# Low-weight passes of a unit gathered behind its other passes, with TensorE's wait for the low weights moved there

## The chip, the cores and the metric

One NeuronCore of a Trainium2 chip runs the whole program in one launch. The metric is the time on the device in microseconds, the median of the runs. The engines named in this document are TensorE (PE; its weight loads have rows of their own, PEld), VectorE (DVE), ScalarE (ACT), GpSimd (POOL) and SyncE (SP), which starts the transfers of the weights.

## What is computed

Two transformer blocks in fp32, on 256 tokens of width 1024. The first is a feed-forward block, a mixer (sparse attention and an S5 scan side by side), a second feed-forward block and a gated embedding. The second has two layers, each with a retention, a gated MLP and a differential attention between `w_in` and `w_out`; its first layer also carries 256 context tokens, so that many of its products have 512 columns.

```python
def swiglu(x, w1, w3, w2):
    return (jax.nn.silu(x @ w1) * (x @ w3)) @ w2
...
    # first_block
    h = h + 0.5 * swiglu(rmsnorm(h, norm_ffn1[i]), ffn1_w1[i], ffn1_w3[i], ffn1_w2[i])
    z = rmsnorm(h, norm_mix[i]) @ w_in[i]
    ...
    h = h + jnp.concatenate([o_nsa, o_s5], axis=-1) @ w_out[i]
    h = h + 0.5 * swiglu(rmsnorm(h, norm_ffn2[i]), ffn2_w1[i], ffn2_w3[i], ffn2_w2[i])
    gate = jax.nn.sigmoid(rmsnorm(h, norm_ple[i]) @ w_ple_gate[i])
    h = h + gate * (p[i] @ w_ple[i])
    ...
    # second_block, each layer l
    h = modulate(x, g_pre[l], shift, scale)
    rk_, rv_, dk_, dv_, rq_, rg_, dq_, dg_, mu_, mv_, mg_, mlog_ = split_cols(h @ w_in[l], IN_SIZES)
    ...
    out = merge_branches(o_ret, o_mlp, o_diff, mlog_, w_branch_out[l], w_out[l])
    x = x + gate * rms_norm(out, g_post[l])
```

The feed-forward width is 2816, so each feed-forward block has 22 columns of tiles f.

## The kernel before

**Units.** All weights come as a stream of 359 units of 128 x 1024 fp32 (512 KB); a unit is eight 128 x 128 tiles, and `stream_plan` gives their order. In a feed-forward block that is w1 and w3 of column f = 0, then for each f the w1 and w3 of f + 1 and the w2 of f. SP loads unit u into slot u % 4 of `ring` (four slots) and waits for that until PE has multiplied unit u - 4 (`units_multiplied`, raised by the last matmul of a unit).

**Three passes.** For 347 of the units, the split ones, an fp32 product is made of three passes with fp32r operands. ACT copies the unit into its high part `w_hi` (`high_part`, L1290; three slots; it waits for the load and for the multiplying of the split unit three before). DVE then subtracts, `w_lo` = `ring` - `w_hi` (`low_part`, L451; it waits for the high part and raises `lo_ready`). The input is likewise kept as a high and a low part: `hn` (high part on ACT at L1365 or L1575, low part on DVE at L1897 or L2309) and `hid` in the feed-forward (`hid_hi` on ACT, `hid_lo` at L2015 on DVE). `exact` (L518 to L525) gives the three passes of a tile one after the other: `w_hi` x high input, `w_hi` x low input, `w_lo` x high input. A unit is thus 24 passes, of 256 or 512 columns.

**PE's waits.** Before a unit PE waits for its low part (`split_unit`, L512 to L516), and so implicitly for its high part:

```python
def split_unit(name, body=0):
    who, count = LOW[name]
    pe.wait_ge(lo_ready[who], count + body)
    return w_parts(name)
```

**Order of work.** PE's order is that of the stream. ACT's order of high parts (`part`, `prepare`) and DVE's of low parts are written out by hand between their other steps: on DVE in a feed-forward block as `part(3 * f + 2)`, `gated`, `part(3 * f + 3)`, `gated_low`, with steps of the S5 tables (L1937 to L1975) and of the modulation (`mod_junk`, L1919) between them, and elsewhere as `low_until(name)`, which makes all low parts up to the named unit. `modulated` (L2300) is the loop over the eight tiles of a normalised input: L2306 scales a tile, ACT makes its high part (`hn_hi`), L2309 its low part (`hn_lo`); its argument `lows` names a tile behind which a low part of weights is made. It is called with `{7: ("dk", l, 2)}` for layer 0 and with `{5: ("dq", l, 2)}` for layer 1. `head_sum` puts a small product between two tiles of `project2`.

**Where the three passes are used.** `up` and `down` in the feed-forward blocks (and `first_up` for their first two units), `project` for the projections of block 1, the units `wout`, `context_half`, `residual_halves`, `project2` for the projections of block 2 (`ctx_by_tile` for one unit that waits for its input tile by tile), and the units `wbo` and `wo` at the end of each layer.

## Time and profile before

| | |
|---|---|
| median of 3 runs | 1518.09 us (1516.82 to 1519.3) |
| profiled execution | 1522.82 us, span 1521.1 us |
| mean granted TensorE clock in it | 0.996 |
| PE busy | 1465.7 us (96%), 10,040 matmuls |
| DVE busy | 959.2 us (63%) |
| ACT busy | 721.5 us (47%) |
| transfers | 223.25 MB, mean 147 GB/s |
| chain that ended last | PE 80%, DVE 8%, DMA 6%, ACT 4% |

A row of the timeline gives the start, the duration, engine, line and operation, then what is written and what is read, and in brackets the idle time of the engine before it with what ended it. The ends of matmuls are modelled: the distance between two starts says more than a duration. The execution goes through feed-forward 1 (to 212 us), the projections and the mixer (to 364), feed-forward 2 (to 554), the gated embedding and the change to block 2 (to 620), and the two layers of block 2, of which the second begins at about 1150.

### The profile page before, as it was taken

How to read it: one execution, taken by the hardware profiler on the slowest of the kernel's cores; microseconds unless marked ns; L12 is line 12 of the kernel's file. 1: busy time of each engine (PE TensorE's matmuls, PEld its weight loads, DVE VectorE, ACT ScalarE, POOL GpSimd, SP SyncE). 2: the span in 40 equal slices, each digit the busy share in tenths (PEclk: the TensorE clock that was granted, in tenths of full speed). 3: DMA queues.
4: the chain of work that ended last, by engine and by line, in shares of the span. 5: the costliest groups of instructions: out<-in, count | busy, mean ns of one | idle time of the engine just before them, and what ended most of it. 6: DMA issues, size and time to landing. Idle time of an engine off the chain costs nothing.

```text
span 1521.1 us, 25975 instructions
## 1 busy us (share of the span) xinstructions
PE 1465.7 (96%) x10040; PEld 1304.4 (86%) x10040; DVE 959.2 (63%) x1522; ACT 721.5 (47%) x1252; POOL 80.6 (5%) x129
## 2 busy tenths in 40 slices
PE   6999999989999999999999999999999999999997
PEld 6999999769999988787778788888888887889997
DVE  5778788767666678865654447664246635557665
ACT  5444466366444457327545353222245435556444
POOL 4600000000000000001001000000000002010000
PEclk9999999999999999999999999999999999999999
DMA  7766645516666644442222123543332332225663
GB/s 277 236 197 194 211 134 199 176 49 228 223 211 207 217 159 147 159 159 77 70 70 70 56 83 133 177 134 111 101 108 97 99 124 77 83 94 180 210 206 130
DMA packets 71033, 223.25 MB, mean 147 GB/s; under 512 B 6688, under 2 KB 21024, under 8 KB 70432
## 3 DMA queue, kind: packets, MB, share of 16 engines
q1 hardware_dynamic: 54528, 194.67, 38.7%
q10 hardware_dynamic: 16416, 27.34, 5.4%
q8 instruction: 62, 1.02, 0.3%
q14 instruction: 27, 0.22, 0.0%
HBM read 220.94 MB, written 1.05 MB: 146 GB/s over the span
## 4 chain that ended last, share of the span: by engine, by line
PE 80%; DVE 8%; DMA 6%; ACT 4%; issue 2%; SPq 0%; DVEq 0%; ACTq 0%
PE ps L524 67%; DMA ring<-stream 5%; DVE w_lo L451 3%; ACT w_hi L1290 2%; PE ps L539 1%; PE ps L1029 1%; PE ps L1045 1%; PE ps L1037 1%; DVE mod_junk L1919 1%; PE ps L1113 1%; PE ps L1102 1%; PE ps L1002 1%; PE ps L1082 0%; DMA pk<-pack 0%; PE ps L1062 0%
## 5 line engine op out<-in xcount | busy, mean ns | idle before, releaser
L524 PE MATMUL ps<-hn_hi,w_hi 128*128 128x256 f32 (+1 forms) x1895 | 603.3, 318 | 17.2 <-DVE w_lo L451 9.8
L451 DVE TENSOR_TENSOR w_lo<-ring,w_hi 128x1024 fp32r<-128x1024 f32 (+1 forms) x347 | 415.1, 1202 | 283.2 <-ACT w_hi L1290 279.5
L524 PE MATMUL ps<-hn_hi,w_lo 128*128 128x256 f32 (+1 forms) x1895 | 589.5, 311 | 0.0
L524 PE MATMUL ps<-hn_lo,w_hi 128*128 128x256 f32 (+1 forms) x1895 | 589.1, 311 | 0.0
L1290 ACT ACTIVATE w_hi<-ring 128x1024 fp32r<-128x1024 f32 (+1 forms) x347 | 360.2, 1039 | 339.5 <-DMA ring<-stream 263.6
L524 PEld LDWEIGHTS ps<-hn_hi,w_hi 128*128 128x128 f32 x1895 | 359.1, 189 | 47.1 <-DVE w_lo L451 15.5
L524 PEld LDWEIGHTS ps<-hn_lo,w_hi 128*128 128x128 f32 x1895 | 360.1, 190 | 20.7 <-issue 0.5
L524 PEld LDWEIGHTS ps<-hn_hi,w_lo 128*128 128x128 f32 x1895 | 358.3, 189 | 21.3
L1359 ACT ACTIVATE area<-ps 128x512 f32<-128x512 f32 (+1 forms) x136 | 67.1, 508 | 209.3 <-PE ps L524 209.0
L524 PE MATMUL ps<-area_r,w_hi 128*128 128x256 f32 (+1 forms) x578 | 132.1, 323 | 0.9 <-ACT area L1359 0.6
L524 PE MATMUL ps<-hid_hi,w_hi 128*128 128x256 f32 x352 | 99.3, 282 | 6.5 <-DVE w_lo L451 5.2
L524 PEld LDWEIGHTS ps<-area_r,w_hi 128*128 128x128 f32 x578 | 95.9, 188 | 11.1 <-DVE w_lo L451 1.1
L524 PE MATMUL ps<-hid_lo,w_hi 128*128 128x256 f32 x352 | 97.7, 278 | 0.0
L524 PE MATMUL ps<-hid_hi,w_lo 128*128 128x256 f32 x352 | 97.7, 277 | 0.0
L524 PE MATMUL ps<-area_r,w_lo 128*128 128x256 f32 (+1 forms) x289 | 92.7, 321 | 0.0
L524 PE MATMUL ps<-w_hi,hn_hi 128*128 128x512 f32 (+1 forms) x192 | 77.3, 402 | 0.0
L524 PEld LDWEIGHTS ps<-hid_hi,w_hi 128*128 128x128 f32 x352 | 66.2, 188 | 8.8 <-issue 6.0
L524 PE MATMUL ps<-w_lo,hn_hi 128*128 128x512 f32 (+1 forms) x192 | 73.4, 382 | 0.0
L524 PE MATMUL ps<-w_hi,hn_lo 128*128 128x512 f32 (+1 forms) x192 | 73.3, 382 | 0.0
L524 PEld LDWEIGHTS ps<-hid_hi,w_lo 128*128 128x128 f32 x352 | 66.2, 188 | 0.0
L524 PEld LDWEIGHTS ps<-hid_lo,w_hi 128*128 128x128 f32 x352 | 66.2, 188 | 0.0
L524 PEld LDWEIGHTS ps<-area_r,w_lo 128*128 128x128 f32 x289 | 54.3, 188 | 4.5
(328 smaller groups left out, 1568.1 us busy)
## 6 DMA issues: line engine op xcount, KB each, us to landing
ring<-stream SPq DMA_DIRECT2D x359, 512.0 KB, 3.8
mod_at<-mod_stream ACTq DMA_DIRECT2D x24, 512.0 KB, 5.4
area<-mod_stream ACTq DMA_DIRECT2D x22, 512.0 KB, 4.9
pk<-pack ACTq DMA_DIRECT2D x1, 1610.0 KB, 7.2
pk<-pack SPq DMA_DIRECT2D x1, 1549.0 KB, 12.2
h<-x_in SPq DMA_DIRECT2D x1, 1024.0 KB, 4.8
cond_at<-cond SPq DMA_DIRECT2D x2, 512.0 KB, 14.2
mod_at<-mod_stream SPq DMA_DIRECT2D x2, 512.0 KB, 12.5
```

What stands on the lines that cost most here:

```text
L451: eng.tensor_tensor(lo[:, 0:w], raw, hi[:, 0:w].bitcast(F32), ALU.subtract).then_inc(lo_ready[who], 1)
L524: m = pe.matmul(dst, w_, x_, start=(start and n == 0), stop=(stop and n == 2), skip_group_check=True)
L539: m = pe.matmul(bank(b, 0, tokens), c("ones"), src, start=(k == first), stop=(k == KT - 1), skip_group_check=True)
L1002: m = pe.matmul(ps[:, 4 * 512 + T * j:4 * 512 + T * j + T], c("rot64" if part[0] == "d" else "rot128"), z[:, a0 + j, 0:T], start=(j % 2 == ...
L1029: pe.matmul(bank(4 + m_, T * st, 2 * T - T * st), diffz[rows, 4 + hh, q0:q0 + P], diffz[rows, hh, keys], start=True, stop=True).then_inc(s ...
L1037: m = pe.transpose(bank(6, P * kt, P), aux[:, 4 + n % 2, P * kt:P * kt + P], c("ident"))
L1045: m = pe.matmul(bank(7, P * qt, P), diffv[:, kt, P * hh:P * hh + P], aux[:, 6 + n % 2, P * kt:P * kt + P], start=(kt == 2 * st), stop=(kt ...
L1102: m = pe.matmul(bank(4 + n % 2, T * kt, T), retz[:, hh, T * st + P * kt:T * st + P * kt + P], retz[:, 4 + hh, T * st:T * st + T], start=(k ...
L1113: m = pe.matmul(bank(6 + n % 2, 0, T), retv[:, 2 * st + kt, P * hh:P * hh + P], aux[:, n % 2, T * kt:T * kt + T], start=(kt == 0), stop=(s ...
L1290: act.activation(w_parts(name)[0][:, 0:w], ring[:, u % RING, PLACE:PLACE + w], ACT.Copy).then_inc(hi_ready, 1)
L1359: act.activation(dst, bank(BANK[name][0], 0, tokens), func, **kw).then_inc(act_evac, 1)
L1919: stt(quarter(mod_junk[:, :].bitcast(BF16)), w, 1.0, silu(0), ALU.mult, ALU.mult, accum_out=out_at(0)).then_inc(s("mod_half"), 1)
```

## The change

For 259 of the 347 split units PE no longer waits for the low part at the head. It waits for the high part (`high_unit`), gives the two passes with `w_hi` for all eight tiles (`high_passes`), then waits for the low part (`low_unit`) and gives the eight passes with `w_lo` (`low_pass`). These are the units of `up` and `down` (128), those of `project`, `wout` from 2 on and `pleg`, `context_half`, and those of `project2` but for the one with `ctx_by_tile`. `first_up`, `residual_halves`, `wbo`, `wo` and the units in which the input is the stationary operand stay as they are. On DVE the low part of ("dk", 0, 2) and that of ("dq", 1, 2) are moved from inside the two `modulated` loops to behind them. `head_sum` stands behind as many passes as before. The hunks for `wout` and `context_half` are like that of `project` and left out here.

```diff
@@ -515,6 +515,26 @@
                 pe.wait_ge(lo_ready[who], count + body)
                 return w_parts(name)
 
+            def high_unit(name, body=0):
+
+                pe.wait_ge(hi_ready, SPLIT[name] + 1 + body)
+                return w_parts(name)
+
+            def low_unit(name, body=0):
+
+                who, count = LOW[name]
+                pe.wait_ge(lo_ready[who], count + body)
+
+            def high_passes(dst, weights, wcols, x, xcols, start):
+
+                for n in range(2):
+                    m = pe.matmul(dst, weights[0][wcols], x[n][xcols], start=(start and n == 0), stop=False, skip_group_check=True)
+                return m
+
+            def low_pass(dst, weights, wcols, x, xcols, stop):
+
+                return pe.matmul(dst, weights[1][wcols], x[0][xcols], start=False, stop=stop, skip_group_check=True)
+
             def exact(dst, weights, wcols, x, xcols, start, stop, x_stationary=False):
...
@@ -560,18 +580,26 @@
 
                 def up(f, body=0):
                     for half, w in enumerate(("w1", "w3")):
-                        wt = split_unit((tag, w, f), body)
+                        wt = high_unit((tag, w, f), body)
                         for k in range(KT):
-                            m = exact(bank(4 + f % 4, T * half, T), wt, (all_p, slice(P * k, P * k + P)),
-                                      hn, (all_p, k, slice(0, T)), k == 0 and half == 0, k == KT - 1)
+                            high_passes(bank(4 + f % 4, T * half, T), wt, (all_p, slice(P * k, P * k + P)),
+                                        hn, (all_p, k, slice(0, T)), k == 0 and half == 0)
+                        low_unit((tag, w, f), body)
+                        for k in range(KT):
+                            m = low_pass(bank(4 + f % 4, T * half, T), wt, (all_p, slice(P * k, P * k + P)),
+                                         hn, (all_p, k, slice(0, T)), k == KT - 1)
                         m.then_inc(units_multiplied, 1)
 
                 def down(f, body=0, hidden=0):
-                    wt = split_unit((tag, "w2", f), body)
+                    wt = high_unit((tag, "w2", f), body)
                     pe.wait_ge(hidden_ready, FT * n_ffn + f + 1 + hidden)
                     for j in range(KT):
-                        m = exact(bank(j // 2, T * (j % 2), T), wt, (all_p, slice(P * j, P * j + P)),
-                                  hid, (all_p, f % 4, all_t), f == 0 and j % 2 == 0, f == FT - 1)
+                        high_passes(bank(j // 2, T * (j % 2), T), wt, (all_p, slice(P * j, P * j + P)),
+                                    hid, (all_p, f % 4, all_t), f == 0 and j % 2 == 0)
+                    low_unit((tag, "w2", f), body)
+                    for j in range(KT):
+                        m = low_pass(bank(j // 2, T * (j % 2), T), wt, (all_p, slice(P * j, P * j + P)),
+                                     hid, (all_p, f % 4, all_t), f == FT - 1)
                     m.then_inc(units_multiplied, 1)
...
@@ -603,16 +631,18 @@
             def project(name, tokens=T, cols=None, kt=KT, src=None):
 
                 split = name in SPLIT
-                wt = split_unit(name) if split else unit(name)
+                wt = high_unit(name) if split else unit(name)
                 bank_free(pe, name)
-                b = BANK[name][0]
-                for k in range(kt):
-                    if split:
-                        m = exact(bank(b, 0, tokens), wt, (all_p, slice(P * k, P * k + P)), hn, (all_p, k, slice(0, tokens)),
-                                  k == 0, k == kt - 1)
-                    else:
-                        m = pe.matmul(bank(b, 0, tokens), wt[:, P * k:P * k + P], src[:, k, 0:tokens],
-                                      start=(k == 0), stop=(k == kt - 1))
+                o = bank(BANK[name][0], 0, tokens)
+                if split:
+                    for k in range(kt):
+                        high_passes(o, wt, (all_p, slice(P * k, P * k + P)), hn, (all_p, k, slice(0, tokens)), k == 0)
+                    low_unit(name)
+                    for k in range(kt):
+                        m = low_pass(o, wt, (all_p, slice(P * k, P * k + P)), hn, (all_p, k, slice(0, tokens)), k == kt - 1)
+                else:
+                    for k in range(kt):
+                        m = pe.matmul(o, wt[:, P * k:P * k + P], src[:, k, 0:tokens], start=(k == 0), stop=(k == kt - 1))
                 m.then_inc(units_multiplied, 1)
...
@@ -963,15 +999,26 @@
 
 
             def project2(name, l, tokens, ctx_by_tile=False):
-                wt = split_unit(name)
+                wt = high_unit(name)
                 bank_free(pe, name)
                 o = bank(BANK[name][0], 0, tokens)
-                for k in range(KT):
-                    if ctx_by_tile:
+                if ctx_by_tile:
+                    low_unit(name)
+                    for k in range(KT):
                         pe.wait_ge(s("ctx_modulated"), KT * l + k + 1)
-                    m = exact(o, wt, (all_p, slice(P * k, P * k + P)), hn, (all_p, k, slice(0, tokens)), k == 0, k == KT - 1)
-                    if k == (3 if tokens > T else 5):
-                        head_sum()
+                        m = exact(o, wt, (all_p, slice(P * k, P * k + P)), hn, (all_p, k, slice(0, tokens)), k == 0, k == KT - 1)
+                        if k == 3:
+                            head_sum()
+                else:
+                    for k in range(KT):
+                        high_passes(o, wt, (all_p, slice(P * k, P * k + P)), hn, (all_p, k, slice(0, tokens)), k == 0)
+                        if tokens > T and k == 5:
+                            head_sum()
+                    low_unit(name)
+                    for k in range(KT):
+                        m = low_pass(o, wt, (all_p, slice(P * k, P * k + P)), hn, (all_p, k, slice(0, tokens)), k == KT - 1)
+                        if tokens <= T and k == 1:
+                            head_sum()
                 m.then_inc(units_multiplied, 1)
...
@@ -2463,12 +2510,13 @@
                 tok = 2 * T if l == 0 else T
                 dve.wait_ge(mods_ready, 4 + 3 * l)
                 if l == 0:
-                    modulated(0, 0, h, lambda k: gamp[:, k:k + 1], aux[:, 9, T:2 * T], {7: ("dk", l, 2)})
+                    modulated(0, 0, h, lambda k: gamp[:, k:k + 1], aux[:, 9, T:2 * T])
+                    low_until(("dk", l, 2))
                     final_norm()
                 else:
                     low_until(("dq", l, 1))
                     dve.wait_ge(s("x_rstd"), 2)
-                    modulated(1, 0, h, lambda k: amp[:, 1, k, 0:1], rstd[:, 0:T], {5: ("dq", l, 2)})
+                    modulated(1, 0, h, lambda k: amp[:, 1, k, 0:1], rstd[:, 0:T])
                     low_until(("dq", l, 3))
```

## Rows read from the trace of the kernel before

**Rows 1.** Busy time by engine, share of the span, instructions: the page.

```profile
PE 1465.7 (96%) x10040; PEld 1304.4 (86%) x10040; DVE 959.2 (63%) x1522; ACT 721.5 (47%) x1252; POOL 80.6 (5%) x129
```

**Rows 2.** PE's waits (us, times, longest): 0:212, 212:364, 364:554, 554:620, 1150:1521.

```profile
PE ps L524 <- DVE w_lo L451: 5.3, 8, 1.7
PE ps L524 <- DVE hid_lo L2015: 1.1, 1, 1.1
...
PE ps L524 <- DVE w_lo L451: 1.4, 2, 1.0
...
PE ps L524 <- DVE w_lo L451: 3.6, 7, 0.8
...
PE ps L524 <- DVE w_lo L451: 2.8, 4, 1.0
PE ps L524 <- DVE hn_lo L2309: 1.8, 1, 1.8
...
PE ps L524 <- DVE w_lo L451: 2.0, 4, 0.8
PE ps L524 <- DVE hn_lo L2309: 1.4, 1, 1.4
```

**Rows 3.** Groups by shape: busy, mean ns, idle time before and its releasers.

```profile
L451 DVE TENSOR_TENSOR w_lo<-ring,w_hi 128x1024 fp32r<-128x1024 f32 x331 | 404.4, 1227 | 261.7 <-ACT w_hi L1290 258.0
...
L1290 ACT ACTIVATE w_hi<-ring 128x1024 fp32r<-128x1024 f32 x331 | 350.1, 1059 | 325.7 <-DMA ring<-stream 254.2 <-PE ps L524 61.7 <-issue 9.1
```

**Rows 4.** Timeline of PE, 67 to 76 us (start, duration, work, idle before).

```profile
67.23 0.28 PE L524 MATMUL ps<-hid_hi,w_lo 128*128 128x256 f32 x1
...
67.84 0.38 PE L524 MATMUL ps<-hn_hi,w_hi 128*128 128x256 f32 x1 [0.33 <-DVE w_lo L451]
68.06 0.29 PE L524 MATMUL ps<-hn_lo,w_hi 128*128 128x256 f32 x1
...
70.57 0.28 PE L524 MATMUL ps<-hn_hi,w_lo 128*128 128x256 f32 x1
70.68 0.28 PE L524 MATMUL ps<-hn_hi,w_hi 128*128 128x256 f32 x1
...
75.30 0.38 PE L524 MATMUL ps<-hid_hi,w_hi 128*128 128x256 f32 x1 [1.74 <-DVE w_lo L451]
```

**Rows 5.** Chain of waits, 60 to 130 us (start, duration, what).

```profile
81.39 4.44 DMA ring<-stream
85.86 1.07 ACT w_hi L1290
```

**Rows 6.** Timeline of DVE, 66 to 77 us.

```profile
66.56 1.23 DVE L451 TENSOR_TENSOR w_lo<-ring,w_hi 128x1024 fp32r<-128x1024 f32 x1 [2.18 <-ACT w_hi L1290]
...
73.21 0.69 DVE L1975 TENSOR_SCALAR area<-area 128x1024 f32<-128x1024 f32 x1
```

**Rows 7.** Timeline of PE, 50 to 51.2 us.

```profile
50.80 0.28 PE L524 MATMUL ps<-hn_hi,w_lo 128*128 128x256 f32 x1
50.92 0.28 PE L524 MATMUL ps<-hn_hi,w_hi 128*128 128x256 f32 x1
```

**Rows 8.** Timeline of PE, 208 to 209 us.

```profile
208.62 0.39 PE L524 MATMUL ps<-hid_hi,w_hi 128*128 128x256 f32 x1 [0.85 <-DVE w_lo L451]
```

**Rows 9.** Timeline of ACT, 205 to 232 us.

```profile
212.43 2.54 ACT L1272 ACTIVATE area<-h 128x256 f32<-128x256 f32 x8
```

**Rows 10.** Busy times in one stretch, then granted clock, DMA share, GB/s.

```profile
601.20:604.60 3.40, 3.40 (x18) 3.40 (x17) 3.06 (x9) 2.77 (x5) 0.00 (x0) 0.50 0.79 317
```

**Rows 11.** Timeline of DVE, 1160 to 1166 us.

```profile
1163.26 1.22 DVE L451 TENSOR_TENSOR w_lo<-ring,w_hi 128x1024 fp32r<-128x1024 f32 x1 [0.34 <-ACT w_hi L1290]
```

**Rows 12.** Timeline of DVE, 603 to 608 us.

```profile
605.93 1.22 DVE L451 TENSOR_TENSOR w_lo<-ring,w_hi 128x1024 fp32r<-128x1024 f32 x1
```

**Rows 13.** Timeline of ACT, 611 to 614 us.

```profile
612.68 1.05 ACT L1290 ACTIVATE w_hi<-ring 128x1024 fp32r<-128x1024 f32 x1
```

**Rows 14.** Weight loads of PE, 70.3 to 70.9 us.

```profile
70.57 0.19 PEld L524 LDWEIGHTS ps<-hn_hi,w_hi 128*128 128x128 f32 x1
```

More of the change, by code:

```diff
@@ L906, in _ @@
             for j in range(2, KT):
-                wt = split_unit(("wout", j))
+                wt = high_unit(("wout", j))
                 bank_free(pe, ("wout", j))
                 for k in range(KT):
-                    m = exact(bank(BANK["wout", j][0], 0, T), wt, (all_p, slice(P * k, P * k + P)),
-                              hn, (all_p, k, slice(0, T)), k == 0, k == KT - 1)
+                    high_passes(bank(BANK["wout", j][0], 0, T), wt, (all_p, slice(P * k, P * k + P)), hn, (all_p, k, slice(0, T)), k == 0)
+                low_unit(("wout", j))
+                for k in range(KT):
+                    m = low_pass(bank(BANK["wout", j][0], 0, T), wt, (all_p, slice(P * k, P * k + P)),
+                                 hn, (all_p, k, slice(0, T)), k == KT - 1)
                 m.then_inc(units_multiplied, 1)
@@ L944, in context_half @@
                 for k in range(KT):
-                    exact(bank(BANK[name][0], T, T), wt, (all_p, slice(P * k, P * k + P)),
-                          hn, (all_p, k, slice(T, 2 * T)), k == 0, k == KT - 1)
+                    high_passes(bank(BANK[name][0], T, T), wt, (all_p, slice(P * k, P * k + P)), hn, (all_p, k, slice(T, 2 * T)), k == 0)
+                low_unit(name)
+                for k in range(KT):
+                    low_pass(bank(BANK[name][0], T, T), wt, (all_p, slice(P * k, P * k + P)),
+                             hn, (all_p, k, slice(T, 2 * T)), k == KT - 1)
             def residual_halves(names):
@@ L965, in project2 @@
             def project2(name, l, tokens, ctx_by_tile=False):
-                wt = split_unit(name)
+                wt = high_unit(name)
                 bank_free(pe, name)
                 o = bank(BANK[name][0], 0, tokens)
-                for k in range(KT):
-                    if ctx_by_tile:
+                if ctx_by_tile:
+                    low_unit(name)
+                    for k in range(KT):
                         pe.wait_ge(s("ctx_modulated"), KT * l + k + 1)
-                    m = exact(o, wt, (all_p, slice(P * k, P * k + P)), hn, (all_p, k, slice(0, tokens)), k == 0, k == KT - 1)
-                    if k == (3 if tokens > T else 5):
-                        head_sum()
+                        m = exact(o, wt, (all_p, slice(P * k, P * k + P)), hn, (all_p, k, slice(0, tokens)), k == 0, k == KT - 1)
+                        if k == 3:
+                            head_sum()
+                else:
+                    for k in range(KT):
+                        high_passes(o, wt, (all_p, slice(P * k, P * k + P)), hn, (all_p, k, slice(0, tokens)), k == 0)
+                        if tokens > T and k == 5:
+                            head_sum()
+                    low_unit(name)
+                    for k in range(KT):
+                        m = low_pass(o, wt, (all_p, slice(P * k, P * k + P)), hn, (all_p, k, slice(0, tokens)), k == KT - 1)
+                        if tokens <= T and k == 1:
+                            head_sum()
                 m.then_inc(units_multiplied, 1)
```

## The prediction

> **What bounds the kernel now.** I read the page's busy times first [rows 1]. TensorE (PE) is busy for 1465.7 of 1521.1 us, so whatever the change can win lies in the 55 us in which PE is idle, or in the pace of its passes. Next come the waits of PE, one answer for each stage [rows 2]. Every row "w_lo L451" is PE standing at the head of a weight unit for its low part: 5.3 + 1.4 + 3.6 + 2.8 + 2.0 = 15.1 us in 8 + 2 + 7 + 4 + 4 = 25 waits; between 620 and 1150 us there is none. The other rows are two waits for the low part of the input (hn_lo L2309) and one for hid_lo. The third view is the groups by shape [rows 3]: making a high part takes ACT 1.06 us, and the low part takes VectorE (DVE) another 1.23 us after it, since the subtraction reads the high part.
>
> What a wait costs is more than its idle figure, because the ends of matmuls are modelled. At 67.23 the last pass of a unit starts, and at 67.84 the next [rows 4]: 0.61 us where two passes are 0.11 us apart, so 0.50 is lost though the row says 0.33. The following start is at 68.06, 0.22 later and not 0.11: the restart takes another 0.11. So a wait costs its idle time plus 0.17 plus 0.11, about 0.27 us more than listed. All 25 together: 15.1 + 25 x 0.27 = 21.9 us. That is the pot.
>
> The chain of waits shows where such a wait comes from [rows 5]: once a unit has left the ring, the load of the next takes 4.44 us, and its high part follows at 85.86 for 1.07 us; the low part comes behind that. DVE has two sorts of delay [rows 6]: it is in other work when the high part is ready (73.21 is a table step, and only behind it comes the low part for which PE waits until 75.30), or the high part itself is just done (66.56, idle before, released by w_hi). In the second sort PE loses at most the 1.23 us of the low part.
>
> **The change part by part.** *Low part asked for 16 passes later.* A unit has 24 passes. In 259 of the 347 split units (128 of the two feed-forward blocks, 24 of the other projections before block 2, 107 of block 2) the first 16 now need only the high part. At 0.113 to 0.118 us a pass for 256 columns [rows 4, 7] the low part may now be 1.8 to 1.9 us later than before, at 512 columns 3.6 us later. The largest listed wait is 1.7 idle [rows 2], so 2.0 in all: nearly all waits fit under the new allowance. The number of passes, their columns, the weight loads, the order of units and the moment at which a unit is released are unchanged; a unit is released by its last pass as before, and the DMA queue of SP, which waits for that, sees the same order. Where PE now waits in the middle of a unit, what stands behind it are 8 passes and, at the end, the release that frees a ring slot, so a late low part delays the load four units on as it does today.
>
> *High part asked for at the head.* It is ready 1.2 us or more ahead of the low part. I take each stage by itself (idle + 0.27 a wait):
> - Feed-forward 1, to 212 us: 5.3 + 8 x 0.27 = 7.5. The last of its waits (208.62, idle 0.85, so 1.1 in all [rows 8]) brings nothing: ACT begins the squares at 212.43 with no idle before them [rows 9], so ACT is the bound there, and PE needs the squares. Around 75.30 DVE is held by its table steps, so I leave 0.5 there. 5.9 remain. The hid_lo wait (1.1) stays, since hid_lo stands behind the same low part on DVE.
> - 212 to 364: 1.4 + 2 x 0.27 = 1.9, of which I take 1.7 (0.3 of it stands ahead of ACT and DVE chains of the attention, which keep their length).
> - Feed-forward 2, 364 to 554: 3.6 + 7 x 0.27 = 5.5, all of it; the units before and behind are on time.
> - 554 to 620: 2.8 + 4 x 0.27 = 3.9. Here DVE is the rival bound: PE already waits 1.8 us for hn_lo [rows 2], at 600.89, so arriving earlier there mostly makes this wait longer. Behind it lies a stretch in which the granted clock is 0.50 [rows 10], the lower of the two levels (1.2 GHz), in which 18 passes take 3.40 us; it came after that idle time and would stay, since the idle time does.
> - From 1150: 2.0 + 4 x 0.27 = 3.1; the last of the four (0.2 idle, so 0.5) stands before a unit whose order isn't changed, and I leave another 0.3. I take 2.3.
>
> *Low parts taken out of the two normalisation loops.* At 1163.26 DVE makes the low part of a later unit between two tiles of hn_lo [rows 11], and PE waits 1.4 us for the next tile [rows 2]. The step takes 1.22 us; ACT has its own high part in between, so 1.2 comes back, with the low part then made behind the loop and needed 16 passes later. At 605.93 it is the same for the last tile of the other loop [rows 12], but PE is then still at the tiles before it, so I take 0.3, a quarter of the step. Behind it the unit at 615.04 needs its high part, which ACT makes from 612.68 to 613.73 [rows 13] behind DVE steps that keep their length: with the low part waiting in the middle, PE could start there at most 1.3 earlier, and this takes the place of the 0.3. With an estimated 0.8 where PE sums squares earlier, the stage brings 2.1 of its 3.9. Cover of this edit: DVE does the same steps in all; without the 16 passes of cover each low part would cost its 1.23 us again.
>
> *The extra wait itself.* 259 units get one wait more. Lower end: zero, and not below, since a met wait removes nothing: as between two units of one kind when the semaphore is already there: starts at 70.57 and 70.68, 0.11 apart, across a unit's end [rows 4]. Upper end: a full restart, 0.107 us, 259 times = 27.7 us. I take zero: it is the same situation, one wait on one semaphore in front of a weight load. The Trainium skill's page "TensorE: Matmul & The Clock Gate" (Part 2, step by step) says that weight loads are pulled ahead of the matmuls in flight. A wait in front of a load could stop that, and the sum by that reading would be 18.7 - 27.7 = -9.0. By this trace the load for the pass at 70.68 starts at 70.57 [rows 14], together with the pass before it, so there loads go on being pulled ahead past a met wait.
>
> *Pace.* Passes of 256 columns run at two paces: 0.113 (70.57 to 70.68 [rows 4]) and 0.118 (50.80 to 50.92 [rows 7]), and stay in one until a unit's end. Of the intervals between starts on L524 (the rows of its timeline from 15.28 on), 2,194 are at most 0.115 us and 3,139 are 0.116 to 0.119, with means of 0.1134 and 0.1178. All three kinds of pass keep whichever pace the unit has, so I see no reason for a shift by their order. Bounds: all at the fast one -3,139 x 0.0044 = -13.8 us; all at the slow one +2,194 x 0.0044 = +9.7. I take zero and keep a part of both ends.
>
> **Sum.** 5.9 + 1.7 + 5.5 + 2.1 + 2.3 + 1.2 = 18.7 us. The profiled execution took 1522.8 us (span 1521.1), so 1504.1 there; the median of the runs shown is 1518.1, 4.7 lower, and the same subtraction gives **1499.4 us**.
>
> **Rivals.**
> - *The next thing is late.* Where PE comes sooner, ACT or the DMA is what it meets. A load takes 4.44 us and the high part 1.07 [rows 5]; a slot is refilled three units ahead of its use, 3 x 24 x 0.113 = 8.1 us, so 2.6 us are spare. For it: a fifth of ACT's idle time ahead of high parts is no wait for a load (325.7 in all, 254.2 for loads) [rows 3], and several stages hang on ACT. If half of the pot comes back, 21.9 / 2 = 11, the time is 1507.
> - *Pace moves in our favour.* Mid-unit there is no switch between w_hi and w_lo any more, and half of the slow passes could turn fast: 7 us more, 1492. Against it: nothing in the rows ties pace to the kind of pass.
> - *Each mid-unit wait is a restart.* Mechanism: the wait drains the queue of loads even when it is met; place: between pass 16 and 17 of each of the 259 units. 27.7 - 18.7 = +9.0, so 1527. It decides from 0.072 us per unit (18.7 / 259). For it: the restart of 0.107 is real after a wait that was not met. Against it: 70.57 to 70.68 [rows 4, 14].
> - *It doesn't do what it says*: the waits move to the middle of the unit instead of vanishing, because DVE falls behind by what PE gains. Then 1515 to 1520. Against it: DVE stands idle for 258.0 us waiting for high parts [rows 3].
>
> **How the numbers follow.** Forecast (13 to 22 us won) 0.55; next thing late (4 to 13) 0.20; pace in favour (over 22) 0.12; restarts or a slower pace, above 1521 0.07; no effect 0.06. About 0.2%, 3.0 us, is what a measurement here can tell from no change. Faster by more than that: 0.55 + 0.20 + 0.12 = 0.87; within 0.06; slower 0.07. Range: forecast, the better part of "late" and most of the pace case, 1490 to 1512, leaves about 2 in 10 outside.
>
> **What would show it.** In the changed profile: PE's waits for w_lo fall from 25 to a handful, all in front of a pass hn_hi,w_lo; the wait at 600.89 grows to 3 us or more; the hn_lo wait of the 1150 stage all but goes; in a unit whose low part is ready, passes 16 and 17 start 0.11 to 0.12 apart (0.22 would be the restart rival); the counts of the two paces stay. Wrong it would be if new waits for w_hi L1290 of several us appear, or if the mean of the low passes rises by itself.

## The result, and the profile after

| | before | changed |
|---|---|---|
| median | 1518.07 us (1516.82 to 1519.3, 4 runs) | 1503.04 us (1502.62 to 1503.81, 4 runs) |
| profiled execution | 1522.82 us, span 1521.1 | 1502.62 us, span 1500.8 |

The ratio is 0.9902, with a 95% interval of 0.9885 to 0.9919: the change takes 15.0 us off the median. Between the two profiled executions the difference is 20.3 us of span: the profiled run of before lay 4.7 us above its median, that of the changed kernel 0.4 below its own.

In the changed kernel the two passes with `w_hi` have line L531, the low passes L536, the units left in the old order L544, the sums of squares L559; the low parts of the weights are still made at L451, the high parts now at L1337, `hid_lo` at L2062, `hn_lo` at L1944 and L2356. From the page of the changed kernel: its span, the busy times, the chain by engine, and the low passes as a group.

```profile
span 1500.8 us, 25976 instructions
PE 1456.7 (97%) x10040; PEld 1300.7 (87%) x10040; DVE 957.8 (64%) x1522; ACT 720.6 (48%) x1252; POOL 85.3 (6%) x129
PE 88%; DVE 5%; ACT 3%; DMA 2%; issue 1%; DVEq 0%; SPq 0%; ACTq 0%
...
L536 PE MATMUL ps<-hn_hi,w_lo 128*128 128x256 f32 (+1 forms) x1720 | 291.7, 312 | 0.5 <-DVE w_lo L451 0.5
```

PE is busy 97% of the time instead of 96 [rows 1]; the chain goes through PE for 88% of the span instead of 80, and through DVE for 5% instead of 8. Behind the low passes, 1,720 of them in this group, PE idled for 0.5 us.

PE's waits over the whole span (us in total, times, longest), those that answer to [rows 2]:

```profile
PE ps L559 <- ACT area L1319: 4.0, 2, 2.4
PE ps L544 <- DVE hn_lo L2356: 2.3, 3, 1.8
PE ps L531 <- ACT w_hi L1337: 1.6, 2, 0.8
PE ps L531 <- DVE hid_lo L2062: 1.5, 2, 0.8
PE ps L536 <- DVE w_lo L451: 0.5, 1, 0.5
PE ps L544 <- DVE w_lo L451: 0.2, 1, 0.2
```

The 25 waits for w_lo, 15.1 us, have become one of 0.5 us in the middle of a unit and one of 0.2 in a unit of the old order. The waits for hn_lo in the two loops, 3.2 us together before, are 2.3 us. New are two waits for a high part, 1.6 us. The waits for squares on ACT, 4.0 us here, were 2.5 in the same two places in the trace of before, and those for hid_lo, 1.5 us in two places, were 1.1 in one.

Rows of PE's timeline of the changed kernel (start, duration, work, idle before):

```profile
69.96 0.28 PE L531 MATMUL ps<-hn_lo,w_hi 128*128 128x256 f32 x1
70.08 1.11 PE L536 MATMUL ps<-hn_hi,w_lo 128*128 128x256 f32 x8
71.02 0.29 PE L531 MATMUL ps<-hid_hi,w_hi 128*128 128x256 f32 x1
...
204.93 1.35 PE L559 MATMUL ps<-area,pk 128*128 128x256 f32 x5 [2.39 <-ACT area L1319]
...
572.11 1.12 PE L559 MATMUL ps<-area,pk 128*128 128x512 f32 x2 [1.07 <-DVE area L1933]
...
585.89 0.39 PE L544 MATMUL ps<-hn_hi,w_hi 128*128 128x256 f32 x1 [1.83 <-DVE hn_lo L2356]
...
599.05 0.50 PE L531 MATMUL ps<-hn_hi,w_hi 128*128 128x512 f32 x1 [0.83 <-ACT w_hi L1337]
...
1148.21 0.39 PE L544 MATMUL ps<-hn_hi,w_hi 128*128 128x256 f32 x1 [0.25 <-DVE hn_lo L2356]
...
1162.57 0.97 PE L536 MATMUL ps<-hn_hi,w_lo 128*128 128x256 f32 x6 [0.53 <-DVE w_lo L451]
```

At 69.96 the sixteenth pass of a unit starts, and at 70.08 the first low one: 0.12 us across the added wait. The other rows are where PE now waits, in the order of time.

**Where the time went.** Each last matmul of a unit raises a semaphore, so the ends of all units can be set beside each other in two traces; they stand in no row of the page and were taken from the traces' semaphore records. The lead of the changed kernel over the profiled run of before is 1.15 us at the first unit (the start, before any changed unit), 9.09 at the end of feed-forward 1, 7.95 at the first unit of the mixer (1.15 lost again in front of the squares), 9.65 at `wout` 4, 14.93 at the end of feed-forward 2, 16.01 at the first units of block 2, 16.01 still at 1150 us, 18.99 at about 1180 and 20.3 at the end. The 1.15 us of the start is not the change's: the first unit ends at 22.15 us in this profile of the changed kernel and at 23.48 in its second one, at 23.30 and at 22.36, 23.41 and 22.18 in the four of before.

### The profile page after: what moved, and what is told of

It is laid out like the page before. It is cut to its first block, busy times and chain, and to the rows that moved or that the text cites. A ratio compares the mean times of both kernels' runs of the same rounds, so it can differ in the third digit from the quotient of the medians.

```text
span 1500.8 us, 25976 instructions
## 1 busy us (share of the span) xinstructions
PE 1456.7 (97%) x10040; PEld 1300.7 (87%) x10040; DVE 957.8 (64%) x1522; ACT 720.6 (48%) x1252; POOL 85.3 (6%) x129
## 4 chain that ended last, share of the span: by engine, by line
PE 88%; DVE 5%; ACT 3%; DMA 2%; issue 1%; DVEq 0%; SPq 0%; ACTq 0%
PE ps L531 37%; PE ps L544 21%; PE ps L536 18%; DMA ring<-stream 1%; PE ps L1076 1%; PE ps L559 1%; PE ps L1092 1%; ACT w_hi L1337 1%; DVE w_lo L451 1%; PE ps L1084 1%; PE ps L1160 1%; PE ps L1149 1%; PE ps L1049 1%; PE ps L1129 0%; DMA pk<-pack 0%
## 5 line engine op out<-in xcount | busy, mean ns | idle before, releaser
L451 DVE TENSOR_TENSOR w_lo<-ring,w_hi 128x1024 fp32r<-128x1024 f32 (+1 forms) x347 | 415.1, 1202 | 268.1 <-ACT w_hi L1337 263.8
L1337 ACT ACTIVATE w_hi<-ring 128x1024 fp32r<-128x1024 f32 (+1 forms) x347 | 360.1, 1039 | 330.0 <-DMA ring<-stream 243.7
L531 PE MATMUL ps<-hn_hi,w_hi 128*128 128x256 f32 (+1 forms) x1720 | 495.5, 317 | 2.7 <-ACT w_hi L1337 1.6
L531 PE MATMUL ps<-hn_lo,w_hi 128*128 128x256 f32 (+1 forms) x1720 | 486.0, 311 | 0.0
L531 PEld LDWEIGHTS ps<-hn_hi,w_hi 128*128 128x128 f32 x1720 | 324.2, 188 | 25.7 <-issue 4.3
L531 PEld LDWEIGHTS ps<-hn_lo,w_hi 128*128 128x128 f32 x1720 | 324.4, 189 | 19.4 <-issue 0.7
L536 PE MATMUL ps<-hn_hi,w_lo 128*128 128x256 f32 (+1 forms) x1720 | 291.7, 312 | 0.5 <-DVE w_lo L451 0.5
L536 PEld LDWEIGHTS ps<-hn_hi,w_lo 128*128 128x128 f32 x1720 | 247.4, 189 | 20.5 <-DVE w_lo L451 0.7
L544 PE MATMUL ps<-area_r,w_hi 128*128 128x256 f32 (+1 forms) x578 | 132.0, 323 | 0.7 <-ACT area L1406 0.4
L544 PEld LDWEIGHTS ps<-area_r,w_hi 128*128 128x128 f32 x578 | 95.9, 188 | 10.6 <-DVE w_lo L451 0.8
L544 PE MATMUL ps<-area_r,w_lo 128*128 128x256 f32 (+1 forms) x289 | 92.7, 321 | 0.0
L531 PE MATMUL ps<-hid_hi,w_hi 128*128 128x256 f32 x352 | 83.0, 278 | 1.5 <-DVE hid_lo L2062 1.5
L531 PE MATMUL ps<-hid_lo,w_hi 128*128 128x256 f32 x352 | 82.5, 277 | 0.0
L544 PE MATMUL ps<-w_hi,hn_hi 128*128 128x512 f32 (+1 forms) x192 | 77.3, 402 | 0.0
L544 PE MATMUL ps<-w_lo,hn_hi 128*128 128x512 f32 (+1 forms) x192 | 73.4, 382 | 0.0
L544 PE MATMUL ps<-w_hi,hn_lo 128*128 128x512 f32 (+1 forms) x192 | 73.3, 382 | 0.0
L531 PEld LDWEIGHTS ps<-hid_hi,w_hi 128*128 128x128 f32 x352 | 66.1, 188 | 1.9 <-issue 0.9
L531 PEld LDWEIGHTS ps<-hid_lo,w_hi 128*128 128x128 f32 x352 | 66.3, 188 | 0.0
L544 PE MATMUL ps<-hn_hi,w_hi 128*128 128x256 f32 (+1 forms) x175 | 55.1, 315 | 5.3 <-DVE hn_lo L1944 2.9
L544 PEld LDWEIGHTS ps<-area_r,w_lo 128*128 128x128 f32 x289 | 54.3, 188 | 4.4
L1325 ACT ACTIVATE lnr<-ps,eps 128x256 f32<-128x256 f32 x34 | 16.1, 473 | 79.4 <-PE ps L1109 48.1
```

Of the source, the lines that this page charges most:

```text
L451: eng.tensor_tensor(lo[:, 0:w], raw, hi[:, 0:w].bitcast(F32), ALU.subtract).then_inc(lo_ready[who], 1)
L531: m = pe.matmul(dst, weights[0][wcols], x[n][xcols], start=(start and n == 0), stop=False, skip_group_check=True)
L536: return pe.matmul(dst, weights[1][wcols], x[0][xcols], start=False, stop=stop, skip_group_check=True)
L544: m = pe.matmul(dst, w_, x_, start=(start and n == 0), stop=(stop and n == 2), skip_group_check=True)
L1325: link(act.activation(lnr[:, col:col + tokens], src, ACT.Ln, bias=eps[:, 0:1], scale=1.0 / width))
L1337: act.activation(w_parts(name)[0][:, 0:w], ring[:, u % RING, PLACE:PLACE + w], ACT.Copy).then_inc(hi_ready, 1)
```

## Experiments

Each kernel stands beside runs of the kernel before from its own chip and its own comparison. The ratio is not always the quotient of the two medians: for the kernels below the two can be 1 us apart, so a gain is given by both where it matters.

**Order or wait.** The first three kernels have the same order of passes and differ only in where PE asks for the low part: ahead of pass 1, of pass 9 or of pass 17 (the changed kernel itself).

```diff
             def high_unit(name, body=0):
 
-                pe.wait_ge(hi_ready, SPLIT[name] + 1 + body)
+                who, count = LOW[name]
+                pe.wait_ge(lo_ready[who], count + body)
                 return w_parts(name)
 
             def low_unit(name, body=0):
 
-                who, count = LOW[name]
-                pe.wait_ge(lo_ready[who], count + body)
+                pass
```

> The changed kernel with its order of passes and its two moved low parts, but PE waits for the low part at the head of each unit, as before. Theory (the gain is the cover of 16 passes in front of the wait): 1516.5 to 1518.5, at most 1.5 us below before, and the waits for w_lo are back at 20 to 27. Rival (the order of passes itself brings the gain, by pace or by loads of the same tile following one another): 1503 to 1506.

Measured: 1517.96 us beside 1519.92 of before, ratio 0.9994 (0.9979 to 1.0008), with a highest run of 1522.43. The order of the passes alone, with the two moved low parts, can't be told from no change, and is far from the rival's 1503 to 1506. Its waits for w_lo:

```profile
PE ps L531 <- DVE w_lo L451: 11.7, 19, 1.7
PE ps L544 <- DVE w_lo L451: 0.2, 1, 0.2
```

They are back, 20 of them. The two kernels differ in nothing but the place of the wait, so the gain is the wait's, not the order's.

```diff
                         for k in range(KT):
+                            if k == 4:
+                                low_unit((tag, w, f), body)
                             high_passes(bank(4 + f % 4, T * half, T), wt, (all_p, slice(P * k, P * k + P)),
                                         hn, (all_p, k, slice(0, T)), k == 0 and half == 0)
-                        low_unit((tag, w, f), body)
```

(and so in `down`, `project`, `wout`, `context_half` and `project2`)

> The changed kernel with the wait for the low part in front of the ninth pass of a unit (behind tile 3's high passes) and not in front of the seventeenth; the order of the passes is that of the changed kernel. Theory: a cover of 8 passes, 0.91 us at 256 columns. Of the losses in the profile of before only four were longer than that where the low part was what PE needed: 1.90, 1.19, 1.10 and 0.99 us, of which 0.98, 0.27, 0.18 and 0.07 would be left, each with a restart of 0.11: 1.9 us. So 1504 to 1505.5. Rival (each unit loses in proportion to how early it waits): half of the 15 us, 1510 to 1511.

Measured: 1506.25 us beside 1519.92, ratio 0.9917 (0.9896 to 0.9937): with half of the cover 13.7 us of gain by the medians and 12.6 by the ratio, and no run above 1508.25, so the rival's 1510 to 1511 is out. What is left of the waits, and the largest of them:

```profile
PE ps L531 <- DVE w_lo L451: 2.2, 4, 0.6
...
72.72 0.38 PE L531 MATMUL ps<-hid_hi,w_hi 128*128 128x256 f32 x1 [0.63 <-DVE w_lo L451]
```

Four waits, 2.2 us listed and 3.3 with 0.27 each, where 1.9 were expected. The ends of the units show them: they fall behind those of the changed kernel by 0.9 us at 75, 0.4 at 225 and 0.8 at 570, three of the four losses named, and by 0.8 at 1160 in place of the one of 0.99; another 1.4 lies at 215, behind a half-clock stretch at 205.8. The time is 0.8 above the range; before is 1.9 above its first median in this comparison. Cover is worth what it spans of each wait, and with 0.9 us most of the waits are already gone: a wait of 0.6 us and one of 1.9 are both "a wait for the low part", but only the second needs the other eight passes.

**The added waits.**

```diff
                         low_unit((tag, w, f), body)
                         for k in range(KT):
+                            low_unit((tag, w, f), body)
                             m = low_pass(bank(4 + f % 4, T * half, T), wt, (all_p, slice(P * k, P * k + P)),
```

> The changed kernel with its wait for the low part repeated in front of each of the eight low passes, 259 x 8 = 2,072 more waits, all of them met when they are reached. Theory (a met wait costs nothing): within 2 us of the changed kernel, and starts of low passes stay 0.11 to 0.12 us apart. Rival (a met wait drains the loads, the price at which the prediction's restart case would have decided is 0.072 us): 2,072 x 0.072 = 149 us more, at a full restart of 0.107 us 222 us more.

Measured: 1503.56 us beside 1518.69, ratio 0.9897 (0.9882 to 0.9911): the gain of the changed kernel, 15.1 us, is all there. From its page and its waits:

```profile
span 1502.3 us, 26242 instructions
...
PE ps L536 <- DVE w_lo L451: 0.3, 1, 0.3
```

The span is 1.5 us above that of the changed kernel, against the 149 or 222 us of the restart case; by the ends of the units 1.7 us are lost at 217, behind a half-clock stretch at 206.1. In the trace, starts of low passes of 256 columns are 116.4 ns apart on the mean, in the changed kernel 116.3 (the few above 130 ns left out), and a weight load starts 3 ns behind the start of the pass before it in both, with a wait on it or without. So a met wait in front of a weight load costs under a nanosecond, even if the whole 1.5 us is put down to the 2,072 of them.

The page has 26,242 instructions where that of the changed kernel has 25,976, 266 more and not 2,072. In the trace all 2,072 low loads carry a wait of their own, and 259 instructions are new at the line of `low_unit`, one for each unit: a single wait rides on the weight load, and only in front of the first low pass, where two now stand, is there an instruction of its own. The other 7 belong to the unit with `ctx_by_tile`, where the edit put 8 more waits beside those for the input tiles. The Trainium skill says that of waits on several engines (Perfetto Trace Analysis, Identifying Dependency Chains: such instructions may have an EventSemaphore instruction put ahead of them); here the 259 came with two waits on one semaphore. The changed kernel against the kernel before, with one wait more per unit, has one instruction more. That settles the restart rival, and with it what I had weighed against the Trainium skill's rule on loads pulled ahead (TensorE: Matmul & The Clock Gate, Part 2, Step-by-step): in this trace met waits don't hold the pull-ahead back.

**The two moved low parts.** Once put back in the changed kernel, once moved alone.

```diff
-                    modulated(0, 0, h, lambda k: gamp[:, k:k + 1], aux[:, 9, T:2 * T])
-                    low_until(("dk", l, 2))
+                    modulated(0, 0, h, lambda k: gamp[:, k:k + 1], aux[:, 9, T:2 * T], {7: ("dk", l, 2)})
...
-                    modulated(1, 0, h, lambda k: amp[:, 1, k, 0:1], rstd[:, 0:T])
+                    modulated(1, 0, h, lambda k: amp[:, 1, k, 0:1], rstd[:, 0:T], {5: ("dq", l, 2)})
```

> The changed kernel with the low parts of (dk,0,2) and (dq,1,2) back inside the two loops. Theory: the loop of layer 1 delays hn_lo by 1.2 us, PE waits 1.4 us there again; the loop of layer 0 costs 0.3: 1.2 to 1.5 us above the changed kernel on the same chip. Rival (with the wait behind 16 passes the place of a low part no longer matters): within 0.4 us of it.

Measured: 1503.9 us beside 1502.67 of the changed kernel on the same chip, with overlapping runs (1502.97 to 1504.76 and 1502.32 to 1506.7) and profiled spans of 1501.2 and 1500.9: the times alone don't decide between the theory and the rival. The trace tells more than the medians. PE's timeline with the low parts in the loops:

```profile
1147.68 0.39 PE L544 MATMUL ps<-hn_hi,w_hi 128*128 128x256 f32 x1 [1.39 <-DVE hn_lo L2356]
```

The wait of 1.4 us for hn_lo is back; in the changed kernel it was 0.25 at 1148.21. By the ends of the units, against the second profile of the changed kernel, this is worth 1.17 us. In layer 0 there is nothing to gain: there the changed kernel gains 0.83 us at ("dk", 0, 0) and has lost 1.07 again at ("dk", 0, 3), whose high part comes late (the wait at 599.05).

The move alone, on the kernel before, is the same diff the other way round:

> The kernel before with nothing but the two low parts moved behind the loops; PE waits at the head and takes the passes tile by tile as before. Theory: hn_lo of the layer 1 loop is 1.2 us earlier, and the low part of (dq,1,2) is made behind the loop and still in time, so 0.5 to 1.5 us below before, which these medians can hardly tell from nothing; in the trace PE's wait for hn_lo L2309 at some 1165 falls from 1.4 to under 0.4. Rival (the move pays only with the cover of 16 passes): the waits for w_lo behind the two loops grow by as much.

Measured: 1517.89 us beside 1518.69, ratio 0.9994 (0.9981 to 1.0006), no difference by the medians, as expected. PE's timeline behind the loop of layer 1, the kernel before first:

```profile
1165.33 0.39 PE L524 MATMUL ps<-hn_hi,w_hi 128*128 128x256 f32 x1 [1.40 <-DVE hn_lo L2309]
1172.58 0.38 PE L524 MATMUL ps<-hn_hi,w_hi 128*128 128x256 f32 x1 [0.76 <-DVE w_lo L451]
1176.13 0.38 PE L524 MATMUL ps<-hn_hi,w_hi 128*128 128x256 f32 x1 [0.56 <-DVE w_lo L451]
1179.67 0.38 PE L524 MATMUL ps<-hn_hi,w_hi 128*128 128x256 f32 x1 [0.54 <-DVE w_lo L451]
...
1160.59 0.39 PE L524 MATMUL ps<-hn_hi,w_hi 128*128 128x256 f32 x1 [0.25 <-DVE hn_lo L2309]
1167.84 0.39 PE L524 MATMUL ps<-hn_hi,w_hi 128*128 128x256 f32 x1 [0.75 <-DVE w_lo L451]
1171.38 0.38 PE L524 MATMUL ps<-hn_hi,w_hi 128*128 128x256 f32 x1 [0.54 <-DVE w_lo L451]
1174.92 0.39 PE L524 MATMUL ps<-hn_hi,w_hi 128*128 128x256 f32 x1 [0.55 <-DVE w_lo L451]
```

The wait for hn_lo fell from 1.4 to 0.25, and the three waits for w_lo behind it kept their size. The move doesn't need the cover of 16 passes.

**The feed-forward alone.** `up` and `down` as in the changed kernel, all else as before.

> Only the 128 units of the two feed-forward blocks are gathered; all else is as before, the two low parts inside the loops included. Theory: by the marks of the unit ends in the two profiles, feed-forward 1 gave 6.8 us (without the start) and feed-forward 2 4.9, so 11.7 of 20.3; the median moved by 15.0, so by the same share 8.6 to 11.7 us, 1506.5 to 1509.5. Rival (the feed-forward's gain depends on what follows): under 5 us, above 1513.

Measured: 1510.55 us beside 1519.92, ratio 0.9946 (0.9926 to 0.9966): 9.4 us by the medians, 8.2 by the ratio. The first is in the range expected (8.6 to 11.7), the second just below it; the time is above its range, since before took 1.9 us more in this comparison. It is 55 to 62% of the whole. The rest was not split by runs; its parts are read from the ends of the units.

**How much there is to lose in a run of before.** The changed kernel and the kernel before, again:

> The changed kernel, unchanged, on the chip of the following runs. Theory: 1502.5 to 1505, 15 us below before, whose runs spread over 8 us, and itself spread over less than 3, because a run can no longer lose the w_lo waits. Rival: as wide a spread as that of before (8 us), if the spread has nothing to do with these waits.

Measured: 1502.67 us beside 1516.96, ratio 0.991 (0.9893 to 0.9927). Four of its five runs lie between 1502.3 and 1502.8, one at 1506.7; the nine of before between 1514.9 and 1520.3. That one run, which has no profile, makes the spread 4.4 us, above the 3 expected, beside 5.4 of before. The other kernels with the late wait spread over 1.8 (e3), 4.7 (e7) and 5.2 us (e9), so it is not shown that the change makes the times steadier.

> The kernel before, unchanged, for a second profile. The changed kernel's span is 20.3 us shorter than that of the first profile of before, but its median is only 15.0 us below the median. Theory: the first profile of before lost some 4.7 us in the pot itself (low parts later than usual), so a second one shows fewer or shorter waits of PE for w_lo, some 11 us listed in place of 15.1. Rival: the 4.7 us lie outside these waits (the start, the pace of the passes, the waits for the statistics), and the w_lo waits come out at 14 to 16 us again.

Measured: 1524.28 us, span 1522.5.

```profile
PE ps L524 <- DVE w_lo L451: 15.9, 26, 1.8
```

The theory failed on this run, and the rival's 14 to 16 us came out: it is slower still than the first profile, and the waits are longer too. So two more followed.

> The kernel before, unchanged, one more profile with its own time. Theory: what a run of before loses in the waits for w_lo differs from run to run, and its time with it: a run below 1518 has under 14 us listed in these waits or one half-clock stretch less (1.7 us each) than the first profile, one above 1521 has 15 or more. Rival: the listed waits are 15 to 16 us whatever the time of the run.

Measured: 1519.27 us, span 1517.5.

```profile
PE ps L524 <- DVE w_lo L451: 14.2, 27, 1.1
```

> The same as the run before it, once more: listed waits for w_lo and half-clock stretches against its own time.

Measured: 1518.38 us, span 1516.7, the run nearest to the median. Neither run lies below 1518 or above 1521, where the theory had put its numbers; the rival's 15 to 16 us whatever the time is out.

```profile
PE ps L524 <- DVE w_lo L451: 12.7, 25, 1.1
```

| run of before | time | waits for w_lo, listed | times | half-clock stretches ahead of the end |
|---|---|---|---|---|
| second | 1524.28 | 15.9 | 26 | 3 |
| first (the prediction's) | 1522.82 | 15.1 | 25 | 2 |
| third | 1519.27 | 14.2 | 27 | 0 |
| fourth | 1518.38 | 12.7 | 25 | 2 |

The four stand in the same order by time and by listed waits. That is weak evidence: the profile of the kernel with only the moved low parts took 1517.8 us with 14.7 us in 24 waits. From the first to the fourth the span falls by 4.4 us, of which 2.4 are the listed waits for w_lo and 1.1 lie ahead of the end of the first unit (23.30 and 22.18 us); the rest was not traced. What there is to win differs from run to run: the wait at 75.30, 1.74 us in the first, is not among those of the fourth, whose longest is 1.1. The half-clock stretches (the granted clock at its lower level) don't follow the time; the kernels with the late wait have none, one or two as well (two in the profile of the changed kernel, none in its second one, with spans of 1500.8 and 1500.9).

**Further along the same road.** What the rows after pointed to was tried on top of the change.

```diff
-                    pe.wait_ge(hidden_ready, FT * n_ffn + f + 1 + hidden)
-                    for j in range(KT):
-                        high_passes(bank(j // 2, T * (j % 2), T), wt, (all_p, slice(P * j, P * j + P)),
-                                    hid, (all_p, f % 4, all_t), f == 0 and j % 2 == 0)
+                    for n, ready in enumerate((s("hid_high"), hidden_ready)):
+                        pe.wait_ge(ready, FT * n_ffn + f + 1 + hidden)
+                        for j in range(KT):
+                            pe.matmul(bank(j // 2, T * (j % 2), T), wt[0][all_p, slice(P * j, P * j + P)],
+                                      hid[n][all_p, f % 4, all_t], start=(f == 0 and j % 2 == 0 and n == 0), stop=False,
+                                      skip_group_check=True)
```

> The changed kernel with the 8 hid_hi passes of a w2 unit first, then the 8 hid_lo passes behind a wait of their own, then the 8 low ones. Theory: the same rule as for the weights (ask for the late operand last): two waits for hid_lo, 1.5 us listed, 1.5 + 2 x 0.27 = 2.0 us with what a wait costs, so 1.5 to 2.0 below the changed kernel on the same chip. Rival: what waits for hid_lo now waits for hid_hi or for the low part, no gain.

Measured: 1500.54 us beside 1502.67 of the changed kernel and 1516.96 of before, ratio to before 0.9893 (0.9876 to 0.9911). No wait for hid_lo is left in its trace. Against the second profile of the changed kernel the ends of the units gain 1.03 us at the first w2 unit and 0.91 at the first of feed-forward 2, which are the two places. The spans of these two profiles differ by 2.1 us, but 1.34 of that is the start, and 0.8 of the gain is lost again behind 1450 us, so their sum fits the medians partly by luck. The runs (1498.93 to 1503.66) overlap with those of the changed kernel: the 2.1 us of the medians are likely and not shown, the 1.9 us in the two places are shown by the traces. Its median is the lowest of the study.

```diff
-            high_parts(2)
             squares(1, h, resid_ready, [k // 2 + 1 for k in range(KT)])
+            high_parts(2)
```

> The kernel e7 with the two high parts that ACT makes ahead of the squares at the end of feed-forward 1 put behind the squares. In the profile of the changed kernel PE waits 2.4 us there for the squares, which begin at 204.48 behind those two high parts (2.00 us), while h is ready from 203.2 on. Theory: the squares start 1.3 to 1.9 us earlier, the root follows 0.3 later than it could: 1.0 to 1.6 us below e7. Rival: the low parts of the units of u then come late by as much, 0.

Measured: 1503.19 us, 2.6 above e7, with runs from 1499.61 to 1504.82, which overlap with those of e7: the expected gain isn't there, and a loss is not shown either. The two profiles (e9's run took 1504.6 us, e7's 1500.54) tell where they part. PE's timeline:

```profile
203.40 0.91 PE L559 MATMUL ps<-area,pk 128*128 128x256 f32 x3 [1.23 <-ACT area L1321]
...
243.64 0.36 PE L531 MATMUL ps<-hn_hi,w_hi 128*128 128x256 f32 x1 [2.23 <-DVE area L2142]
```

The wait for the squares fell from 2.4 to 1.2 us, as expected, and 0.7 of that was left at the first unit of the mixer. Then PE stood 2.2 us at 243.64 for a DVE step (L2142, the rope), a wait that e7 doesn't have. On DVE in between:

```profile
230.52 1.23 DVE L1968 SCALAR_TENSOR_TENSOR mod_junk<-mod_at,cond_at 128x1024 bf16<-128x1024 f32 x1 [0.77 <-DMA mod_at<-mod_stream]
235.09 1.23 DVE L1968 SCALAR_TENSOR_TENSOR mod_junk<-mod_at,cond_at 128x1024 bf16<-128x1024 f32 x1 [0.93 <-DMA mod_at<-mod_stream]
```

DVE waits 0.8 and 0.9 us for weights of the modulation, whose loads ACT starts between its other steps. The e7 trace has neither of these waits, and the rope step L2142 starts there at 240.08 where here it starts at 243.07. So in this run the gain was given back some 40 us later, through work that ACT starts and DVE makes. Another 1.5 us of the difference between the two profiles lies at `wout` 0, behind a half-clock stretch at 307. The rival expected PE to wait for the low parts of u; no such wait is there. Which of ACT's steps came too late was not tried, so this cause is read from the rows and not shown by a run.

## Why the prediction held, and what was off

- **What bounds the kernel.** Right: the gain comes from asking for the low part later, and the order of the passes gave nothing that could be measured (e1). Not all of what the waits cost came back: in the fourth run of before they cost 12.7 + 25 x 0.27 = 19.4 us, and the spans differ by 15.8 with the moved low part in it, because in places another bound stands behind them, as the prediction said.
- **Idle plus 0.27 for a wait.** It held in e7: two waits, 1.6 us listed in the second profile of the changed kernel, make 2.1, and 1.9 came back by the ends of the units. At 75.30, 1.74 + 0.27 = 2.0 was predicted and 2.09 came back.
- **Terms by stage,** against the same profile of before: feed-forward 1 5.9, measured 6.8 (7.95 less the 1.15 of the start); 212 to 364 1.7, measured 1.7; feed-forward 2 5.5, measured 5.3; 554 to 620 2.1, measured 1.1; behind 1150 2.3 + 1.2 = 3.5, measured 3.0 to 1180 and 1.3 behind. In all 19.1 us without the start, for 18.7: nearer than its parts deserve, since 0.9 too little in feed-forward 1 and 1.3 behind 1180, for which there was no term, largely cancel 1.0 and 0.5 too much in the two stages of the loops. The 0.5 that I left at 75.30 was not needed: 16 passes covered all of it. What the last wait of feed-forward 1 was to bring and the squares to take back is in the trace as +1.15 and -1.15, with the wait for the squares grown to 2.39.
- **554 to 620.** I put the loss into the wait for hn_lo at 600.89, which was to grow to 3 us. It stayed at 1.83 (585.89); in its place PE waits 1.07 us at an earlier point, 572.11, for a fold on DVE (L1933) that the squares need, and 0.83 at 599.05 for the high part of ("dk", 0, 3). The bound was DVE as said, the row was another. The 0.3 for the moved low part of layer 0, which did not enter the sum, was wrong (e3: nothing). The half-clock stretch behind this wait, which "would stay", is in neither profile of the changed kernel, and it cost nothing: the first profile of before has it and the third has not, and from 580 to 620 us their unit ends stay 2.7 to 2.8 us apart.
- **The median.** This is the step that was mis-sized, 18.7 for 15.0 us. I took the pot from a profiled run that lay 4.7 us above the median, and subtracted it whole from the median. The pot was itself larger in that run: 15.1 us listed, 12.7 in the run near the median. By the profile of that fourth run and the second one of the changed kernel (from another chip) the spans differ by 1516.7 - 1500.9 = 15.8 us. The row to doubt was in hand: the profiled time stood 4.7 above the median in the same sentence.
- **The extra wait.** Right at zero (e5); the rival needed 0.072 us a unit.
- **Pace.** Of the intervals of 256 columns at most 0.115 us there are 2,037 in place of 2,194, and of 0.116 to 0.119 us 3,366 in place of 3,139: 0.7 to 1.0 us slower. In the second profile of the changed kernel they are 2,129 and 3,267, in the fourth of before 2,115 and 3,241, so most of that shift is the run's and not the change's.
- **The next thing late.** It was there, small: w_hi 1.6 us in two waits, not the half of the pot.

## What to carry to other kernels

Where one operand comes late and the product is a sum of passes, give all passes without it first and wait in the middle: it costs nothing when the operand is there. How much cover is needed is read from the longest waits, not from their sum; here 8 of 16 passes gave 12.6 to 13.7 of 15 us. The waits read from one profiled run belong to that run: where its time lies above the median, don't subtract them whole from the median.

## What the runs showed of the hardware

A wait that is met costs under 1 ns where it rides on a weight load (2,072 of them 1.5 us at most, e5); a second wait on the same load makes an instruction more. Behind a wait that was not met the second pass starts 0.22 us after the first (67.84 and 68.06), where 0.113 is usual [rows 4].

The granted clock fell to half for stretches of 3.41 us with PE at work in them (busy for 3.10 to 3.40 of 3.40 us, in the 18 of them that the 14 profiles have ahead of the end of the program). Here is one behind the longest wait for w_lo in the second run of before, and one behind PE's first wait for hn_lo in the changed kernel; last, a wait of e4 without one. The rows of stretches give busy times, granted clock, DMA share and GB/s:

```profile
73.54 0.38 PE L524 MATMUL ps<-hid_hi,w_hi 128*128 128x256 f32 x1 [1.79 <-DVE w_lo L451]
...
74.20:77.60 3.40, 3.40 (x18) 3.40 (x17) 3.37 (x6) 0.76 (x2) 0.00 (x0) 0.51 0.49 155
...
15.40:18.80 3.40, 3.40 (x18) 3.40 (x17) 3.40 (x10) 2.14 (x6) 2.17 (x6) 0.50 0.99 327
...
59.36 0.38 PE L524 MATMUL ps<-hn_hi,w_hi 128*128 128x256 f32 x1 [1.68 <-DVE w_lo L451]
```

At 74.20, 18 passes ran in 3.40 us, where at 0.113 us a pass there is room for 30: 12 x 0.113 = 1.4 us lost, beside the wait itself. All 18 stretches lie at an idle time of PE of 1.8 us or more (2.75 us at 15, 1.79 at 74, 2.15 or 2.39 at 205, 2.07 at 305 to 314, 1.84 at 587 to 601), and begin between 0.3 us before its end and 1.6 us after. The same idle times had no stretch in other profiles (that of 2.75 us is in all 14 and had one in three), nor had 75.30 in the first profile of before (1.74 us) or 59.36 in e4 (1.68 us): such a wait can cost a stretch at half clock but need not. And a stretch costs nothing where PE waits for another engine soon after, as at 601.2 in the first profile of before.
